# An encoder trunk with grouped experts on one core: the gather of the experts' rows in float32 products, without the split into bfloat16 parts

## What is computed

```python
for l in range(DEPTH):
    x = x + mixer_sublayer(x, norm1_g[l], w_in[l], qk_norm_g[l], na_rpb[l], mix_norm_g[l], w_out[l])
    x = x + hier_moe(rms_norm(x, norm2_g[l]), ...)

# hier_moe, xt: the normalised rows (256 x 1024)
grp = argmax(xt @ w_rg + b_rg)                     # one group of 4
top_v, top_i = top_k(e_logits within grp, 2)       # two of its 8 experts
gate = p_grp * softmax(top_v)
xb = xt[idx]                                       # the rows an expert takes
y = (silu(xb @ w_gate[e]) * (xb @ w_up[e])) @ w_down[e]
out = zeros.at[tok].add(y * gate)
```

## Time and profile before

| what | value |
|---|---|
| median of three runs | 1371.9 us (1371.89 to 1373.58) |
| span of the profiled execution, first to last instruction | 1369.0 us |
| TensorE busy | 1255.0 us, 92% |
| VectorE, ScalarE, GpSimd busy | 360.6, 216.6, 47.4 us |
| DMA | 451.23 MB, mean 330 GB/s, 422 GB/s in the expert stages |
| gather products (L561) busy on TensorE | 104.0 us, 1680 instructions |
| products with expert weights (L576) | 701.6 us |

### The profile page before, as it was taken

The page is one execution under the profiler, slowest core; times in us unless marked ns, Lnnn a source line. Parts: engine busy times, 40 slices in busy tenths (PEclk is TensorE's granted clock), DMA queues, the critical chain, the costliest instruction groups (busy, mean ns, idle before and its releaser), DMA issues.

```text
span 1369.0 us, 17006 instructions
## 1 busy us (share of the span) xinstructions
PE 1255.0 (92%) x6512; PEld 583.3 (43%) x6513; DVE 360.6 (26%) x679; ACT 216.6 (16%) x442; POOL 47.4 (3%) x48
## 2 busy tenths in 40 slices
PE   5998959999999999999699985999999999999987
PEld 3657433433333433333355653433433333433342
DVE  1346251212121212121234625212212212212221
ACT  1126121101011100110111623101110010010000
POOL 1110010000000000000110111000000000000000
PEclk9998969999999999999799986999999999999999
DMA  9950139999999999999933303799999999999991
GB/s 290 345 240 17 41 145 395 421 422 422 422 422 422 422 422 422 422 422 383 339 144 134 138 16 123 294 422 422 421 422 421 422 422 422 423 422 422 422 393 44
DMA packets 81991, 451.23 MB, mean 330 GB/s; under 512 B 12704, under 2 KB 25760, under 8 KB 31264
## 3 DMA queue, kind: packets, MB, share of 16 engines
q1 hardware_dynamic: 81376, 448.60, 80.6%
q0 software_dynamic: 576, 2.10, 0.4%
HBM read 449.63 MB, written 1.05 MB: 329 GB/s over the span
## 4 chain that ended last, share of the span: by engine, by line
issue 57%; PE 36%; POOL 3%; ACT 2%; DVE 2%; DVEq 0%; POOLq 0%; ACTq 0%
PE bank L576 26%; PE bank L610 5%; PE bank L561 4%; POOL rsh L334 1%; ACT work L720 1%; ACT work L734 1%; POOL rstd L334 1%; PE bank L589 0%; POOL work L343 0%; PE bank L417 0%; PE bank L505 0%; DVE hn L789 0%; DVE work L970 0%; POOL work L364 0%; DVE work L817 0%
## 5 line engine op out<-in xcount | busy, mean ns | idle before, releaser
L576 PE MATMUL bank<-ring,work 128*64 128x512 f32 x3168 | 701.6, 595 | 29.7 <-ACT work L734 26.5
L576 PEld LDWEIGHTS bank<-ring,work 128*64 128x64 f32 x3168 | 220.2, 137 | 459.0 <-issue 443.1
L470 PE MATMUL bank<-ring,hT 128*128 128x384 f32 x384 | 125.0, 487 | 2.2 <-DVE rel L872 2.2
L610 PE MATMUL bank<-work 128*128 128x512 f32 x264 | 122.1, 605 | 0.0
L561 PEld LDWEIGHTS bank<-work 128*128 128x128 bf16 x1680 | 98.1, 100 | 37.6 <-issue 37.6
L561 PE MATMUL bank<-work 128*128 128x128 bf16 x1680 | 104.0, 224 | 10.7 <-DVE work L1022 10.7
L1053 DVE COPY work<-bank 128x512 f32<-128x512 f32 x33 | 22.8, 692 | 302.8 <-PE bank L576 302.8
L1058 DVE TENSOR_TENSOR x<-x,bank 128x512 f32<-128x512 f32 x132 | 90.8, 688 | 25.3 <-PE bank L610 24.5
L470 PEld LDWEIGHTS bank<-ring,hT 128*128 128x128 f32 x384 | 72.6, 190 | 52.9 <-DVE rel L872 2.6
L610 PEld LDWEIGHTS bank<-work 128*128 128x128 f32 x264 | 47.4, 189 | 74.1 <-issue 74.1
L1048 DVE TENSOR_TENSOR work<-work,bank 128x512 f32<-128x512 f32 x33 | 22.7, 688 | 199.0 <-PE bank L576 199.0
(11 more groups left out here) (147 smaller groups left out, 645.2 us busy)
## 6 DMA issues: line engine op xcount, KB each, us to landing
ring<-in_w_gate SPq DMA_DIRECT2D x66, 2048.0 KB, 14.2
ring<-in_w_up SPq DMA_DIRECT2D x66, 2048.0 KB, 15.5
ring<-in_w_down SPq DMA_DIRECT2D x66, 2048.0 KB, 16.0
ring<-in_w_in SPq DMA_DIRECT2D x12, 1536.0 KB, 11.6
ring<-in_w_out SPq DMA_DIRECT2D x4, 2048.0 KB, 18.5
x<-in_x SPq DMA_DIRECT2D x1, 1024.0 KB, 5.5
gain<-in_norm_g SPq DMA_DIRECT2D x2, 512.0 KB, 14.1
gain<-in_mix_norm_g POOLq DMA_DIRECT2D x2, 512.0 KB, 3.7
```

The costliest lines, as they stand in the source:

```text
L470: last = nc.tensor.matmul(bank[4 + i][:, 0:HALF_SEG], hT[:, k, t * P:t * P + P], slot8[gi][:, k, c0:c0 + HALF_SEG], start=(k == 0), stop=( ...
L576: last = nc.tensor.matmul(bank[b][e * CAP:e * CAP + CAP, :], lhs[:, k, e * CAP:e * CAP + CAP], weights[s][:, e, k, n * 512:n * 512 + 512], ...
L610: last = nc.tensor.matmul(bank[2 + n][:, :], pickT[:, t, :], y[:, half * 512:half * 512 + 512], start=True, stop=True)
```

## The change

The split is gone with all that fed it: the casts, the subtractions on VectorE and GpSimd, their semaphores and the wait ahead of the first gather. `hn` keeps the normalised rows through the stage. The gather takes its stationary operand from `hn_kc` directly, in float32, and the picks are float32 instead of bfloat16. There are 8 x 2 = 16 products in place of 48.

```diff
@@ -131,8 +131,7 @@
-        xpart = carve(3 * TT * D // 2).bitcast(BF16).rearrange("p (i t k c) -> p i t k c", i=3, t=TT, k=KD)
-        pick = carve(TT * P // 2).bitcast(BF16).rearrange("p (t s) -> p t s", t=TT)
+        pick = carve(TT * P).rearrange("p (t s) -> p t s", t=TT)
...
@@ -359,10 +358,6 @@
-                g.wait_ge(a_part, 3 * l + 3)
-                for t in range(TT):
-                    last = nc.gpsimd.tensor_tensor(xpart[:, 2, t], hn_kc[:, t], xpart[:, 1, t], ALU.subtract)
-                last.then_inc(g_part, 1)
...
@@ -547,7 +542,6 @@
-                pe.wait_ge(g_part, l + 1)
...
@@ -555,12 +549,9 @@
                 for k in range(KD):
-                    n = 0
                     for t in range(TT):
-                        for part in range(3):
-                            last = nc.tensor.matmul(bank[k // 4][:, k % 4 * P:k % 4 * P + P], xpart[:, part, t, k, :],
-                                                    pick[:, t, :], start=(n == 0), stop=(n == 5))
-                            n += 1
+                        last = nc.tensor.matmul(bank[k // 4][:, k % 4 * P:k % 4 * P + P], hn_kc[:, t, k, :],
+                                                pick[:, t, :], start=(t == 0), stop=(t == TT - 1))
...
@@ -703,15 +694,8 @@
-                    act.wait_ge(v_hn, 6 * l + 5 + t)
-                    nc.scalar.copy(xpart[:, 0, t], hn_kc[:, t]).then_inc(a_part, 1)
...
-                act.wait_ge(v_part, l + 1)
-                for t in range(TT):
-                    last = nc.scalar.copy(xpart[:, 1, t], hn_kc[:, t])
-                last.then_inc(a_part, 1)
...
@@ -932,12 +916,6 @@
-                dve.wait_ge(a_part, 3 * l + 2)
-                dve.wait_ge(p_tr, 12 * l + 12)
-                for t in range(TT):
-                    last = tt(hn_kc[:, t], hn_kc[:, t], xpart[:, 0, t], ALU.subtract)
-                last.then_inc(v_part, 1)
```

More of the change, by code:

```diff
@@ L160, in encoder @@
         a_ss, a_hT, a_proj, a_sq, a_q, a_exp, a_pt = (sem("a_" + n) for n in ("ss", "hT", "proj", "sq", "q", "exp", "pt"))
-        a_rexp, a_part, a_silu, a_pickT, a_xg, a_hidT, a_y = (
-            sem("a_" + n) for n in ("rexp", "part", "silu", "pickT", "xg", "hidT", "y"))
+        a_rexp, a_silu, a_pickT, a_xg, a_hidT, a_y = (
+            sem("a_" + n) for n in ("rexp", "silu", "pickT", "xg", "hidT", "y"))
         v_x, v_hn, v_hT, v_proj, v_ssh, v_qk, v_keys, v_soft = (
@@ L165, in encoder @@
         v_rel = sem("v_rel")
-        v_o, v_router, v_chosen, v_flags, v_res, v_part, v_step = (
-            sem("v_" + n) for n in ("o", "router", "chosen", "flags", "res", "part", "step"))
+        v_o, v_router, v_chosen, v_flags, v_res, v_step = (
+            sem("v_" + n) for n in ("o", "router", "chosen", "flags", "res", "step"))
         v_pick, v_pickw, v_xg, v_hid, v_y, v_istep = (sem("v_" + n) for n in ("pick", "pickw", "xg", "hid", "y", "istep"))
         v_back = [sem(f"v_back{n}") for n in range(4)]
-        g_init, g_rstd, g_step, g_keys0, g_part = (sem("g_" + n) for n in ("init", "rstd", "step", "keys0", "part"))
+        g_init, g_rstd, g_step, g_keys0 = (sem("g_" + n) for n in ("init", "rstd", "step", "keys0"))
         seen = [sem(f"seen{i}") for i in range(5)]
```

## The result

| | before | with the change |
|---|---|---|
| median of four runs | 1372.74 us (1371.89 to 1375.04) | 1532.91 us (1530.72 to 1534.07) |
| span of the profiled execution | 1369.0 us | 1531.0 us |

The ratio is 1.116 (95% interval 1.114 to 1.118). The forecast was 1391.6 us with a range that ended at 1408. The time lies far outside it, and nearest to rival 2, the spaced load paid twice (1507 us). One execution of the kernel before, measured beside the later experiments, fell into a slower state of the chip (1714 us, mean granted clock 0.74) and enters no comparison here.

The account below looks back on a forecast made before the run. TensorE was taken to set the pace, with the gather on its path. Items +28.5, heads -9.7 and the repeated pair +0.9 gave +19.7 us on span 1369.0; with 2.9 to the median, 1391.6 us, range 1387 to 1408.

Parts of the forecast that it names:

- rival 2: Gather: the spaced weight load is paid twice, 0.223 us a record, 7.2 us a gather, 1507 us; chance 0.14.
- What bounds the kernel: Expert loop: TensorE sets the pace, and what the gather gains or loses, the 29.3 us item gains or loses.
- Two records a float32 product, and 0.1115 us a record for packed weights: Gather: 16 float32 products as 32 records, spaced as in L521, take 3.74 us, 0.89 us more than before.
- A spaced load is as slow as an ordinary float32 load already is, and not slower on top of it: Gather's weights 32 bytes apart: load stays 0.192 us, as L406 and L521 show, so the step adds nothing.
- The term of 28.5 us: Gathers inside the 32 items: each 0.89 us longer with nothing hiding it, +28.5 us in all.
- The rule from the Trainium skill: SBUF lines are 16 bytes, full rate needs two hits a line; by it alone the new load runs below full rate.
- Head of the stage: Before each layer's first gather: without casts and subtractions, VectorE's picks come 6.16 us sooner.
- First gather: Each layer's first gather, mostly at the lower clock: clock rises after 3.6 us, 5.5 us against 4.17, +1.3 us.
- Transfers: Expert weights need 29.8 us an item; a shorter item would soon be bounded by transfers, a longer one not.
- Rival 4: Gather: one record a float32 product, 1.9 us; item 28.4 us, transfers bind from about the tenth; 1346 us, chance 0.04.

Follow-up runs that it names:

- p1_packed: The changed kernel, with ScalarE copying the normalised rows into a packed float32 tile from which the gather loads its weights; 1394.69 us, ratio to before 1.017.
- two_parts: Kernel before with two bfloat16 parts instead of three, last bits left out, GpSimd subtracting tile by tile ahead of the router; 1332.52 us, ratio 0.969.

## Why the prediction was wrong

- **What bounds the kernel**: right. TensorE set the pace and the gather's time went into the item in full: 5.03 us more a gather, 4.96 more an item.
- **Two records a float32 product, and 0.1115 us a record for packed weights**: right, 0.112 in `p1_packed`. Had the rows been packed, the forecast of 1391.6 would have met 1394.7.
- **"A spaced load is as slow as an ordinary float32 load already is, and not slower on top of it"**: this step failed. It rested on L406, a transpose, which is one record with 32 bytes between its elements and stays at 0.110 us over the few records that the trace has of it. Why a transpose pays so much less stays open. The load of 0.192 us that L406 shares with L521's packed load made them look alike. They aren't: in an ordinary product the step shows in full, 0.238 us a record. The term of 28.5 us was 32 x 5.03 = 161. Rival 2 had the price nearly right, 0.223 for 0.238, and its argument for itself was the sound one: with the load as the limit, any extra shows. The rule from the Trainium skill that stood in the prediction pointed the same way, and was given 0.14. With no ordinary spaced product in the trace, one and the same load time in two kinds of products was too thin for 0.60 on one side.
- **Rival 2's mechanism**, that a load reads its elements twice over, isn't shown. What the steps show is a price that goes with how many elements share 16 bytes. Whether a record reads once or twice stays open, and that 2 x 0.1115 comes near 0.238 may be luck.
- **Head of the stage**: right, 6.07 us for 6.16, with GpSimd as the cause of 4.04 of them. The gather's start at 188.23 instead of 184.9 comes from ahead of the stage.
- **First gather**: the clock rose 3.66 us after its start (forecast 3.6), but it no longer mattered, since a record with the spaced load takes 0.24 us at either level: +3.7 us instead of +1.3. In `p1_packed`, where it matters, the first gathers take 6.50 and 5.45 us, the second as forecast (5.5).
- **Transfers**: "a longer item is not bounded" was right. Rival 4's count, that a shorter item would be bounded from the tenth on, was wrong: `two_parts` ran sixteen with a growing backlog.

## What to carry to other kernels

Before an operand of TensorE is taken from a strided float32 view, look at how many of its elements share 16 bytes: with two or more it costs next to nothing, with one it doubled the record here, for weights and stream alike, unless a longer stream hides the load. A packed copy by an idle engine (two ScalarE copies a layer) turned +160 us into +23, which is still slower than the split that it was to replace. And a small instruction of VectorE that takes ten times its usual time and ends with one of GpSimd's is held up; it is GpSimd's work that has to move.

## What was not expected of the hardware

- The price of a spaced float32 operand is nearly the same at 1.2 and 2.4 GHz (0.240 and 0.238 us a record), while packed records go from 0.213 (L521 in the earlier trace rows) to 0.112 us. It doesn't change with the transfers either (DMA share 0.02 or 1.01).
- 12 bytes cost the mean of the prices at 8 and at 16 bytes, to about 1% (0.174 us).
- Bfloat16 weights 16 and 32 bytes apart cost 0.062 us a record, hardly more than packed (0.056).
- The backlog of transfers reached 33.6 us with four slots before TensorE noticed, at an item of 28.4 us.
